# Gate-up products in another order: how far the plain products run ahead of the others

## What is computed

```python
def swiglu(h, w_gu, w_down):
    g, u = jnp.split(h @ w_gu, 2, axis=-1)
    return (jax.nn.silu(g) * u) @ w_down
```

## Time and profile before

| | us |
|---|---|
| median of three runs | 892.3 |
| the profiled execution | 891.03 |
| its span, first to last instruction | 889.2 |
| TensorE busy, with overlaps counted once | 846.4 |
| VectorE busy | 626.1 |
| ScalarE busy | 374.3 |
| GpSimd busy | 306.1 |

### The profile page before, as it was taken

The page is one execution under the profiler, slowest core; times in us unless marked ns, Lnnn a source line. Parts: engine busy times, 40 slices in busy tenths (PEclk is TensorE's granted clock), DMA queues, the critical chain, the costliest instruction groups (busy, mean ns, idle before and its releaser), DMA issues.

```text
span 889.2 us, 16417 instructions
## 1 busy us (share of the span) xinstructions
PE 846.4 (95%) x6333; PEld 728.1 (82%) x6333; DVE 626.1 (70%) x1232; ACT 374.3 (42%) x754; POOL 306.1 (34%) x303
## 2 busy tenths in 40 slices
PE   3898999999989899999999989999999999999998
PEld 2776788999975667667677989999999999888886
DVE  3457773698758876685759898888999888434434
ACT  1242342221235447668625744444444445322320
POOL 6776100000022314445001167777777772000000
PEclk9899999999997999999999999999999999999999
DMA  8999622264468993961021914333333326222201
GB/s 234 353 372 393 233 64 90 71 216 163 147 230 328 399 370 118 310 181 42 1 65 78 237 49 123 100 96 91 93 92 95 90 95 211 95 95 95 77 1 53
DMA packets 89164, 138.83 MB, mean 156 GB/s; under 512 B 9268, under 2 KB 59988, under 8 KB 84799
## 3 DMA queue, kind: packets, MB, share of 16 engines
q1 hardware_dynamic: 74866, 96.26, 33.6%
q0 software_dynamic: 9376, 40.31, 12.3%
q10 hardware_dynamic: 4844, 1.21, 0.7%
HBM read 130.58 MB, written 11.31 MB: 160 GB/s over the span
## 4 chain that ended last, share of the span: by engine, by line
PE 78%; DVE 7%; DMA 5%; POOL 4%; issue 3%; ACT 3%; SPq 0%; DVEq 0%; ACTq 0%; POOLq 0%
PE bank L2453 19%; PE bank L2455 19%; PE bank L2454 19%; PE bank L2447 4%; POOL arena L894 3%; PE bank L2809 2%; DMA wring<-in_w_ada 2%; PE bank L2521 2%; PE bank L2941 2%; PE bank L2463 2%; PE bank L2462 2%; PE bank L2482 2%; PE bank L2973 2%; PE bank L2779 1%; DMA arena<-in_cache_k_slc,idx 1%
## 5 line engine op out<-in xcount | busy, mean ns | idle before, releaser
L2453 PE MATMUL bank<-s,ring_hi 128*128 128x288 f32 x620 | 184.6, 298 | 3.2 <-DVE ring_lo L537 3.2
L2454 PE MATMUL bank<-s,ring_lo 128*128 128x288 f32 x620 | 183.6, 296 | 0.0
L2455 PE MATMUL bank<-s,ring_hi 128*128 128x288 f32 x620 | 183.1, 295 | 0.0
L2453 PEld LDWEIGHTS bank<-s,ring_hi 128*128 128x128 f32 x620 | 116.9, 189 | 3.9 <-DVE ring_lo L537 3.8
L2455 PEld LDWEIGHTS bank<-s,ring_hi 128*128 128x128 f32 x620 | 117.5, 189 | 0.0
L2454 PEld LDWEIGHTS bank<-s,ring_lo 128*128 128x128 f32 x620 | 117.1, 189 | 0.0
L537 DVE TENSOR_TENSOR ring_lo<-mem,ring_hi 128x512 fp32r<-128x512 f32 x84 | 108.3, 1325 | 0.9 <-POOL mem L990 0.5
L537 DVE TENSOR_TENSOR dn_w<-wring,dn_w 128x2048 fp32r<-128x2048 f32 (+1 forms) x11 | 23.1, 2096 | 65.9 <-ACT dn_w L534 65.9
L903 POOL DMA_INDIRECT arena<-in_cache_k_slc,idx x8 | 7.9, 990 | 159.8 <-PE bank L2455 151.7
L2453 PE MATMUL bank<-dn_w,dn_hi 128*128 128x512 f32 x160 | 62.2, 389 | 0.0
L2454 PE MATMUL bank<-dn_w,dn_lo 128*128 128x512 f32 x160 | 62.2, 389 | 0.0
(11 more groups left out here) (450 smaller groups left out, 2119.3 us busy)
## 6 DMA issues: line engine op xcount, KB each, us to landing
wring<-in_w_gu SPq DMA_DIRECT2D x44, 512.0 KB, 5.2
wring<-in_w_ada SPq DMA_DIRECT2D x16, 1024.0 KB, 10.3
wring<-in_w_in SPq DMA_DIRECT2D x10, 1024.0 KB, 5.2
wring<-in_w_down SPq DMA_DIRECT2D x10, 1024.0 KB, 5.1
wring<-in_w_ada SPq DMA_DIRECT2D x16, 512.0 KB, 8.7
proj<-in_x_prompt SPq DMA_DIRECT2D x4, 512.0 KB, 6.2
mem<-in_state_k_win POOLq DMA_DIRECT2D x8, 256.0 KB, 5.6
mem<-in_state_v_win POOLq DMA_DIRECT2D x8, 256.0 KB, 7.9
```

Of the source, the lines that this page charges most:

```text
L2453: pe.matmul(dst, sh, ml, start=first and k == 0, stop=False)
L2454: pe.matmul(dst, sl, mh, start=False, stop=False)
L2455: ins = pe.matmul(dst, sh, mh, start=False, stop=last and k == len(pairs) - 1)
```

## The change

Only the list `FAST` is built in another way.

```diff
-FAST = [(f, m) for f in range(1, 4) for m in (1, 2)] + [(f, m) for f in range(1, 4) for m in (5, 6, 7, 4, 3)]
-FAST += [(f, m) for f in range(4, NFT) for m in (1, 2, 5, 6, 7, 4, 3)]
+FAST, begun = [], 1
+for f in range(1, NFT):
+    ahead = min(NFT, max(f + 1, f + 3 - (f > 5) - (f > 10) - (f > 15)))
+    FAST += [(x, m) for x in range(begun, ahead) for m in (1, 2)] + [(f, m) for m in (5, 6, 7, 4, 3)]
+    begun = max(begun, ahead)
```

## The result

| | runs | median us | ratio to before (95%) | profiled execution, span |
|---|---|---|---|---|
| before | 6 | 890.74 (888.03 to 893.53) | | 891.03, 889.2 |
| after | 6 | 899.08 (896.93 to 902.18) | 1.0093 (1.0076 to 1.0110) | 898.36, 896.6 |

The account below looks back on a forecast made before the run. TensorE, busy 95% of the span, was taken as the bound, with 4.5 us at most to win. Terms -1.8 + 4.8 + 1.6 + 3.0 = +7.6 us on 891.0 gave 898.6; range 887 to 904, the forecast's own 895.5 to 904.

Parts of the forecast that it names:

- The start: Blocks 1 to 3: wait at (2,3) goes, (2,7) waits 2.05; cost 2.7 in place of 4.5 us, so -1.8.
- the link through the copy: At (2,7): ScalarE's copy waits for block 1's multiplications, VectorE's line 2350 (0.40 us) for the copy, the low part behind.
- The 0.6 at (3,7): Product 7 of block 3: a further wait of 0.6 us, VectorE still being 0.7 late.
- The loads: Weight loads: released 11 us before first cast against 5.2 us to land, so not late; 0 us.
- Blocks 3 to 5 and 7 to 10 as such: Blocks with a turn of seven like the old: zero, bounds 0 and 0.6 for each of blocks 3 to 5.
- (5,7) and (10,7): Product 7 of blocks 5 and 10, where a pair is left out next: waits of 2.4 us each, +4.8.
- the walk: Turn-by-turn timing of VectorE and GpSimd after (4,3): low part of (5,7) ends at 8.9 us, needed at 6.4.
- the nearest rows: Old start's operations, 5.9 us, with line 2350 and a low part: 7.75 after (4,3), a wait of 1.35.
- (7,7) and (12,7): Blocks 7 and 12: walk gave waits of 0.3 and 1.3; half taken, 0.8 us, twice, +1.6.
- The clock: Behind each wait of 2.4 us a fall to 1.2 GHz costing 1.5 us; two, +3.0, none at the start.
- The one that it trades: Rival: waits of 1.35 at (5,7) and (10,7), none at 7 and 12, no clock fall; 891.9 to 895 us; chance 0.22.
- The one that wins: Rival: start's waits go, runs of ten cost nothing, (5,7)'s low part ready by 6.4 us; 886.5 to 890; chance 0.15.

Follow-up runs that it names:

- the run on the copy's link: Kernel after, but ScalarE's copy of a plain product no longer waits for the multiplications three blocks back: 894.99 us, 1.0055 to before.
- The short sums: GpSimd's sums cut to one of four slices, result no longer the layer's: on the kernel before 886.08 us, on the kernel after 887.62 us.
- the single drops: Kernel after, with the lead given back one plain product at a time at blocks 6, 9, 12 and 15: 897.74 us, 1.0074 to before.
- after, late at 9: Kernel after, with the two multiplications that finish block 9 moved behind the low part of (10,7): 895.58 us, one run.
- before, PSUM: Kernel before, with the two multiplications that finish a block taking one input from PSUM: 887.83 us, 0.9956 to before.

## Why the prediction was right

Forecast 898.6, measured 899.08; profiled execution to profiled execution, +7.6 forecast and +7.3 measured. Step by step:

- *The start.* The wait at (2,3) went, the one at (2,7) came: 2.05 forecast, 2.05 measured. The two multiplications both waited for sums, and the link through the copy added its half microsecond, as the run on the copy's link shows. The 0.6 at (3,7) did not come, but the clock fell where I had put no fall. The start cost 3.7 us (2.2 late with the restart, 1.5 clock) for 2.7 forecast. That step was off by 1 us.
- *The loads* cost nothing: no wait of TensorE or VectorE in the stretch names a DMA.
- *Blocks 3 to 5 and 7 to 10 as such*: zero forecast. The kernel after has no wait there but those of the next two points. The run that keeps the lead of two to the end shows one of 0.43.
- *(5,7) and (10,7).* 2.4 forecast, 2.08 and 2.06 measured: the size was 0.3 too high. In the walk the multiplications ended 7.1 us after (4,3); they ended at 567.56, 6.7 after 560.85. The sum from the nearest rows, 5.9 + 0.37 + 1.38, is 7.65 and not 7.75, so by those rows the wait would have been 1.25, further from what was measured. The statement that the copy alters nothing there held: 2.06 with the link freed.
- *(7,7) and (12,7).* 0.8 forecast by halving a walk that gave 1.6; measured 0.68 and 0.69. Halving was a guess that happened to hit.
- *The clock.* Two falls of 1.5 forecast, two measured, but one at the start and only one behind the two long waits. The number was right by luck; the rule behind it was not (see the last section).
- *The sum.* With some 0.15 for each restart, the steps measured -0.8 (forecast -1.8) at the start, 4.4 (4.8) at (5,7) and (10,7), 1.7 (1.6) at (7,7) and (12,7), and 1.5 (3.0) for the clock behind them: 6.8 in all. The other 0.5 of the measured 7.3 us is not placed. The start was too cheap and the clock too dear, and these two errors cancel in good part.
- *The mechanism.* VectorE and GpSimd take turns when both inputs of VectorE's operation lie in SBUF: with one input in PSUM the multiplications take 0.44 and 0.45 us beside sums where they took 1.54. The short sums and the multiplications from PSUM show it from both sides. The Trainium skill, page "SBUF — State Buffer", section "Who interferes with whom", also says that a VectorE operation with at most one SBUF input does not contend with GpSimd; by that, the edit of the multiplications helps though no operation is left out, and the trace agrees (1.54 to 0.45 us).
- *The rivals.* The one that it trades had 1.35 at (5,7) and (10,7) and nothing at 7 and 12; measured were 2.08, 2.06, 0.68 and 0.69, and the time lies above its 895. The one that wins would have needed the low part of (5,7) 6.4 us after (4,3), and it came at 8.4.

What the prediction did not see is in the single drops: I took each block to have about 1 us of rest that a lead could be paid from. There is none. In the middle of the list each product of the lead that is given back costs 1.3 to 1.4 us of waits, singly or in pairs, and more where the copy's link is added. What the lead had won at the start was less: 2.71 us of waits became 2.05.

## What to carry to other kernels

Where two engines take turns on SBUF and both are nearly full, a work order is a fit of gaps: look at what the second engine does during the first one's longest step before moving anything, and walk the turns: a multiplication that had to let a sum finish took 1.54 us in place of 0.45. Running easy work ahead is a loan, and here it was paid back by the product, at 1.3 to 1.4 us each and 2.08 for the first, and more cheaply at the end of the list, where GpSimd had no further sums to make. It is worth more to take operations out of the turns, for instance by leaving an intermediate in PSUM so that only one input lies in SBUF, than to reorder them.

## What the runs showed of the hardware

- The length of a wait alone does not decide whether the clock falls behind it. In the profiled executions of this case 13 waits of TensorE in gate-up were of 2.03 to 2.44 us: behind 7 the granted clock was 0.5 for 3.4 us, behind 6 it stayed at 1.0, the one of 2.37 among these. Each fall came 0.3 to 1.6 us after TensorE had started again, not in the wait. None of the 24 shorter waits, 0.27 to 1.55 us, was followed by a fall. The wait of 2.08 at (5,7) had a fall behind it in the kernel after and none in "after, late at 9", whose order and edits are the same up to there. The Trainium skill, page "TensorE: Matmul & The Clock Gate", section "Part 1: The HAM clock gate (the "warmup" mystery)", says of the rise of the clock at the start of work that it depends on where in the chip's own free-running counting the first matmul lands. A dependence of that kind for the fall would fit these 13 waits, but no run here tests it. So one profile may show such a loss of 1.5 us (an estimate) and another of the same wait none.
- VectorE wrote a result of 128x288 back to PSUM in place at about the cost of writing it to SBUF: 464 and 459 ns on average in 40 instances, against 457 and 454 for the same two operations in the kernel before. These are groups of VectorE's instructions (count, busy us, mean ns) from 520 to 740 us of "before, PSUM".

```profile
L2394 DVE TENSOR_TENSOR bank<-bank,uvT 128x288 f32<-128x288 f32 x20 | 9.3, 464 | 7.1 <-PE bank L2459 7.1
L2390 DVE TENSOR_TENSOR bank<-uvT,bank 128x288 f32<-128x288 f32 x20 | 9.2, 459 | 8.7 <-PE bank L2459 8.7
```
